# VectorE's order in the down projection: low parts, the last convolution tap, residual additions and sums of squares

## The reference

```python
def conv_ffn(x, w_up, conv_w, conv_b, w_down):
    u, g = jnp.split(x @ w_up, [FFN_DIM], axis=-1)     # FFN_DIM = 2816
    g = causal_dwconv(g, conv_w, conv_b)               # 3 taps
    return (jax.nn.gelu(g, approximate=False) * u) @ w_down
...
        ffn = conv_ffn(x, ffn_w_up[i], ffn_conv_w[i], ffn_conv_b[i], ffn_w_down[i])
        x = layer_norm(DEEPNORM_ALPHA * x + ffn, ln_ffn_g[i], ln_ffn_b[i])
        gate = jax.nn.sigmoid(x @ ple_w_gate[i] + ple_b_gate[i])
        x = x + gate * (p[i] @ ple_w_proj[i])
```

## Time and profile before

| | us |
|---|---|
| median of 3 runs (2511.77 to 2514.11) | 2513.59 |
| the profiled execution, its own time | 2513.73 |
| its span in the trace | 2511.8 |
| TensorE busy in the span | 2475.1 (99%) |
| VectorE busy | 1537.9 (61%) |
| ScalarE busy | 1098.0 (44%) |
| GpSimd busy | 1321.7 (53%) |

### The profile page before, as it was taken

The page is one execution under the profiler, slowest core; times in us unless marked ns, Lnnn a source line. Parts: engine busy times, 40 slices in busy tenths (PEclk is TensorE's granted clock), DMA queues, the critical chain, the costliest instruction groups (busy, mean ns, idle before and its releaser), DMA issues. The chain is left out here.

```text
span 2511.8 us, 36104 instructions
## 1 busy us (share of the span) xinstructions
PE 2475.1 (99%) x11658; PEld 2019.5 (80%) x11658; DVE 1537.9 (61%) x2240; ACT 1098.0 (44%) x2016; POOL 1321.7 (53%) x1092
## 2 busy tenths in 40 slices
PE   8999999999999999999999999999999999999999
PEld 5788888888788878888888888777778888878787
DVE  6555552343777775435666666646668777766785
ACT  4333333301766651126777777732432332344442
POOL 3788887433455554432111111154289888666683
PEclk9999999999999999999999999999999999999999
DMA  3222223579210015321111111331133333477552
GB/s 111 88 76 65 68 67 113 176 264 325 76 34 25 27 36 180 131 97 59 43 42 42 42 42 43 122 122 51 47 110 115 118 117 113 137 273 214 180 184 80
DMA packets 126498, 267.24 MB, mean 106 GB/s; under 512 B 13872, under 2 KB 14000, under 8 KB 126400
## 3 DMA queue, kind: packets, MB, share of 16 engines
q1 hardware_dynamic: 84800, 157.85, 19.8%
q10 hardware_dynamic: 41600, 108.19, 12.0%
HBM read 198.02 MB, written 67.96 MB: 106 GB/s over the span
## 5 line engine op out<-in xcount | busy, mean ns | idle before, releaser
L641 POOL TENSOR_SCALAR whi<-raw 128x512 fp32r<-128x512 f32 x194 | 139.5, 719 | 805.5 <-PE bank L869 397.3
L643 POOL TENSOR_TENSOR wlo<-raw,whi 128x512 fp32r<-128x512 f32 x194 | 274.6, 1416 | 16.2
L806 PE MATMUL bank<-a_hi,whi 128*128 128x512 f32 x464 | 184.7, 398 | 1.8 <-issue 1.5
L806 PE MATMUL bank<-b_lo,whi 128*128 128x512 f32 x464 | 183.3, 395 | 0.0
L656 POOL TENSOR_TENSOR wlo<-a,whi 128x512 fp32r<-128x512 f32 x114 | 166.6, 1461 | 18.3 <-ACT whi L1693 17.7
L869 PE MATMUL bank<-b_hi,whi 128*128 128x512 f32 x384 | 157.0, 409 | 0.0
L869 PE MATMUL bank<-b_hi,wlo 128*128 128x512 f32 x384 | 151.5, 395 | 0.0
L869 PE MATMUL bank<-b_lo,whi 128*128 128x512 f32 x384 | 151.2, 394 | 0.0
L806 PE MATMUL bank<-b_hi,whi 128*128 128x512 f32 x336 | 133.3, 397 | 0.4 <-DVE b_lo L2306 0.4
L806 PE MATMUL bank<-a_lo,whi 128*128 128x512 f32 x336 | 132.6, 395 | 0.0
L806 PE MATMUL bank<-a_hi,wlo 128*128 128x512 f32 x336 | 132.6, 395 | 0.0
(11 more groups left out here) (710 smaller groups left out, 7637.5 us busy)
## 6 DMA issues: line engine op xcount, KB each, us to landing
raw<-in_w SPq DMA_DIRECT2D x206, 256.0 KB, 2.6
a<-in_pairs SPq DMA_DIRECT2D x152, 256.0 KB, 2.6
wd_scr<-wd SPq DMA_DIRECT2D x55, 256.0 KB, 4.9
wd<-in_down SPq DMA_DIRECT2D x44, 256.0 KB, 4.5
xs_scr<-made ACTq DMA_DIRECT2D x40, 256.0 KB, 2.6
fc<-c_scr ACTq DMA_DIRECT2D x16, 512.0 KB, 3.7
h_scr<-up_y ACTq DMA_DIRECT2D x13, 512.0 KB, 2.6
raw<-wd_scr SPq DMA_DIRECT2D x26, 256.0 KB, 2.7
```

What stands on the lines that cost most here:

```text
L641: nc.gpsimd.tensor_scalar(hi, src, 1.0, 1.0, ALU.mult, ALU.mult).then_inc(w_hi, 1)
L643: nc.gpsimd.tensor_tensor(lo, src, hi.bitcast(F32), ALU.subtract).then_inc(w_lo, 1)
L806: last = nc.tensor.matmul(psum_ap, ws[w][:, k, :], a[:, kt, hs(h)], start=(first and i == 0 and j == 0), stop=(final and i == n - 1 and j ...
```

## The change

It moves instructions in VectorE's order at two places and adds or removes none. At the first, low parts 9 and 10 (the last of q = 0) go ahead of tap 2 of the last hidden tile. At the second, in q = 5 (products 20 to 23), where the operands of q = 6 (tiles 66 to 76) are made, the additions of squares 1 and 2, low parts 74 and 75, and the additions of squares 3 and 4 go ahead of `down_add(21)`; low part 76 and squares 5 to 7 stand between `down_add(21)` and `down_add(22)`, and `down_add(23)` follows at once. The instructions of all other engines keep their order.

```diff
             tap(FT - 1, 1, up_odd)
             last_sum(last, up_u)
-            operand_lo(range(7, 9))
+            operand_lo(range(7, KD))
             tap(FT - 1, 2, up_odd)
-            operand_lo(range(9, KD))
             dve.wait_ge(sums_out, 7 * NPR)
             gated(FT - 1, up_u_halves, up_odd)
...
             operand_lo(range(first + 3, first + 8))
+            for j in range(1, 3):
+                square_add(n2, 0, j)
+            operand_lo(range(first + 8, first + 10))
+            for j in range(3, 5):
+                square_add(n2, 0, j)
             down_add(5 * NMP + 1)
-            operand_lo(range(first + 8, first + KD))
-            for j in range(1, 4):
+            operand_lo(range(first + 10, first + KD))
+            for j in range(5, KT):
                 square_add(n2, 0, j)
             down_add(5 * NMP + 2)
-            for j in range(4, KT):
-                square_add(n2, 0, j)
             down_add(5 * NMP + 3)
             down_add(6 * NMP)
```

## The result

The changed kernel takes 2520.69 us (median of 13 runs, 2518.47 to 2521.77), the kernel before 2513.79 (13 runs, 2511.77 to 2516.91). The ratio is 1.0025, with a 95% interval of 1.0018 to 1.0032: slower by 0.25%, or 6.9 us (0.27%) by the medians. The profiled execution took 2521.61 us, 7.9 more than that of before, with a span of 2519.7. The forecast was 2518.5, 4.9 us above its base of 2513.59: the direction is the same, and the change 40% larger. The median lies 0.3 us above the upper end of the range, 2520.4; the ratio on the forecast's own base gives 2519.9, inside it.

A forecast was written before the change was run, and what follows sets the result against it. TensorE was taken as the bound, with a matmul in flight almost all the time. Profiled 2513.73 us + 0 (first place) + 3.0 (second place, net) + 1.75 (clock) gave 2518.5 us; range 2515.2 to 2520.4.

The forecast's parts named there:

- What there was to win: TensorE's waits at the two places: 1.65 us for a low part at the first, 2.1 us for GpSimd at the second.
- The first place at 0: Low parts ahead of the last tap: the 1.65 us wait goes, a 1.5 us wait for block 4 comes; net 0.
- my bound of +0.4: First place, upper limit of its cost: +0.4 us, if GpSimd's piece takes 1.79 us and not 1.29.
- The bank at 5.0 us: Second place: product 23 waits 5.0 us for the additions of product 21 to empty its bank; net +3.0 us.
- both collisions: Second place: squares 1 and 4 on VectorE each wait for GpSimd; the additions of product 21 end at 2380.8.
- The clock at 1.75 us: Second place: after the long wait the clock falls to 1.2 GHz, slowing 9 matmuls; 1.75 us.
- a reading of 6.8: Clock at product 23: low stretch of 6.9 us, 4.0 of it inside the wait; 6.8 slow matmuls, 1.3 us.
- one of 12.6: Clock at product 23: low for 5.4 us after work resumes; 12.6 slow matmuls, 2.45 us.
- My first rival: Product 23: the clock stays low longer, 12 or more slow matmuls, near 2519.5 us; chance 0.16.
- The clock always fell: Rival judged here: the clock does not fall after the wait at product 23, 2516.7 us; chance 0.10.
- the bank's wait always bound: Rival judged here: product 23's bank wait does not bind, 2511.6 us, or 2510.0 with the first place; chance 0.03.
- The tap went ahead of GpSimd: Rival at the first place: the last tap runs before GpSimd's piece, gaining 1.3 us, 2517.2 us; chance 0.11.

The follow-up runs named there:

- the mended orders: Against the kernel before: additions of product 21 first, then squares earlier; third try at the second place alone 2512.68 us, with the first place and block 4 earlier 2511.53 us.
- block 4's move: Against the kernel before: the change at the first place alone, plus weight block 4's high part ahead of the last gelu on ScalarE; 2512.84 us.
- The doses of two and four: Against the kernel before: second place only, with two or four instead of six instructions ahead of the additions of product 21; 2516.26 and 2518.09 us.

## Why the prediction came out as it did

- **What there was to win.** I had 1.65 us at the first place and 2.1 at the second. Right: product 1 of the changed kernel starts 8.23 us behind product 0, 9.83 before, and the mended orders give back 2.1 us at the second place.
- **The first place at 0.** Right in two of the three traces of this order (without block 4's move): the place alone measured 0.2 us, with the gelu at the forecast 2205.5 and block 4 at 2209.75. The links were the forecast ones in both traces of the changed kernel, with a tap of 2.3 us; in the trace of the place alone low part 10 met GpSimd and not the tap, so the same end came by another link. In the profiled execution the place cost +2.1, outside my bound of +0.4. The failed step is the bound: I took the landing of operand 10 as fixed (2201.7 for its high part; it was 2200.7, 2201.1 and 2202.5), and I did not ask what the clock does behind the wait for block 4 that I had forecast myself. I had put that wait at 1.5 us, and it was 1.9 us idle.
- **The bank at 5.0 us.** Right: 4.9 us in the changed kernel, 4.8 alone, with both collisions. In the trace of the second place alone the order ran as forecast: low part 74 at 2375.96 (2376.0), square 3 at 2377.17 (2377.2), the additions at 2379.45 (2379.5). Net of the 2.1 us won, 2.8 where I had 3.0. The doses of two and four confirm that the additions' place makes it.
- **The clock at 1.75 us.** The mechanism was right, the size too small: 2.75 us in the profiled execution, 2.4 alone, 2.3 in the second trace of the changed kernel. The term mis-sized is the number of matmuls at the low clock. I took 9, between a reading of 6.8 and one of 12.6; there were 13, 12 and 11. What failed in the lower reading is one assumption, that the clock falls 1.0 us into the wait, as in the one row that I had. The length of the low stretch was right: read in steps of 0.1 us, it was 6.8 us in all three traces. But it began 3.9, 3.0 and 3.0 us into the wait, so that 5.8, 5.1 and 4.8 us of it were left for the matmuls, and not 2.9. Rows of the changed kernel, then of the second place alone (the clock is the third number from the right):

```profile
2381.00:2382.00 1.00, 0.00 (x0) 0.00 (x0) 1.00 (x2) 0.06 (x1) 0.30 (x1) 1.00 0.00 0
2382.00:2384.00 2.00, 0.90 (x2) 0.81 (x3) 1.97 (x4) 1.09 (x2) 0.83 (x1) 0.53 0.45 131
...
2378.00:2380.00 2.00, 0.00 (x0) 0.00 (x0) 2.00 (x2) 0.95 (x2) 0.98 (x1) 0.76 0.08 6
```

One row was too little to go by: at the wait near 1600 us (2.5 us idle before, 2.7 after) the clock fell at 1600.8 in the trace of the kernel before, 1.4 us ahead of the matmuls, and at 1603.9 in that of the changed kernel, 1.2 us behind their start, where it stayed low for 3.4 us only.

- **The sum.** 2518.5 forecast, 2520.69 measured. Of the missing 2.2 us the clock at product 23 is 1.0 in the profiled execution and 0.5 to 0.7 in the other two traces. That the rest is the first place's bad executions is argued and not shown: the profiled one has such a loss, but how often it comes was not counted, the first place alone measured +0.2, and the changed kernel measured again +6.0. My first rival, 12 matmuls or more at the low clock, had a chance of 0.16, and the slower side as a whole 0.36; the profiled execution has 13 such matmuls. I should have given that side the larger share.
- **The other rivals.** The clock always fell at the full dose; the bank's wait always bound. The tap went ahead of GpSimd in none of the three traces: in that of the first place alone it was undisturbed (1.27 us), but only because GpSimd's piece, for which low part 10 had waited, was already done, and that gained nothing.

The Trainium skill's rule (SBUF — State Buffer, "Who interferes with whom"), one path for VectorE and GpSimd held for a whole instruction, is borne out again: two squares' additions took 2.38 us with GpSimd at work (1.4 undisturbed), and the last tap 2.34 us (1.27).

## What to carry to other kernels

An addition that empties a PSUM bank has a due time, the start of the product that writes the bank next: count the slack (here 1.2 us) before anything is put ahead of it. When a wait is taken away, follow the instruction that was moved back instead, through every queue that stands behind it; here each mended order had its next late piece (block 4, block 67, the sum of squares). And do not price a long wait of TensorE by its length alone: behind the five longest in the down projection (1.9 to 4.8 us) the low clock cost 1.6 to 2.8 us more.

## What the runs showed of the hardware

Three things I had not expected. The granted clock fell to 0.50 behind a wait as short as 1.9 us in a dense stream of matmuls, while those of 0.96 to 1.43 us in the down projection left it at 1.00; none between 1.43 and 1.91 us was seen. It may fall after work has resumed: 1.1 us after at the first place, 0.4 us after with four instructions ahead. And what it costs does not follow the wait, but how long the clock stays low and how much of that lies in the wait. It stayed low for 3.4 us at the first place and with four ahead, all of it under matmuls (1.6 and 1.7 us lost), and for 6.8 us in the three traces with six ahead, of which 1.0 to 2.0 us passed in the wait (2.3 to 2.8 us lost). Matmuls that nobody needs, put into the wait, kept the clock at 1.00 and won 2.4 us there.
